# Gate and up products of the inner feed-forward blocks computed with the weights stationary

## The reference, cut to what matters

```
h = rms_norm(x, ffn_norm_w[layer])
gu = h @ w_gate_up[layer]
x = x + (silu(gu[..., :2816]) * gu[..., 2816:]) @ w_down[layer]
```

## Time and profile before

| | |
|---|---|
| three runs | 1253.15, 1253.07, 1252.16 us; median 1253.07 |
| the profiled execution's own time | 1253.0 us |
| its span, first to last instruction | 1251.8 us |
| matmuls on TensorE | 7066, busy 1243.3 us (99%) |
| VectorE, ScalarE, GpSimd | busy 65%, 55%, 11% |
| mean granted TensorE clock | 0.999 of full speed |

### The profile page before, as it was taken

One profiled execution on the slowest core, in us unless ns is written; L12 is line 12 of the kernel. 1 busy time (PEld: TensorE's weight loads), 2 busy tenths in 40 slices (PEclk: granted clock), 3 DMA queues, 4 the chain that ended last, 5 costly groups with the idle time before them and its releaser, 6 DMA issues.

```text
span 1251.8 us, 17456 instructions
## 1 busy us (share of the span) xinstructions
PE 1243.3 (99%) x7066; PEld 1032.8 (83%) x7066; DVE 814.0 (65%) x1114; ACT 691.2 (55%) x1046; POOL 140.8 (11%) x119
## 2 busy tenths in 40 slices
PE   9999999999999999999999999999999999999997
PEld 8888888888888888888888887888888888888886
DVE  5657755566788556655567888846875765755654
ACT  6665644443778645444447755546855363645543
POOL 1130000000221200000000322000320000211112
PEclk9999999999999999999999999999999999999999
DMA  8755466865454648555545534333456544565652
GB/s 296 229 158 185 147 223 202 267 187 164 152 164 157 216 155 253 190 181 178 181 148 188 184 121 150 119 103 102 135 202 235 173 147 133 170 214 171 204 169 85
DMA packets 127697, 220.18 MB, mean 176 GB/s; under 512 B 8336, under 2 KB 71184, under 8 KB 127616
## 3 DMA queue, kind: packets, MB, share of 16 engines
q1 hardware_dynamic: 123360, 205.95, 51.2%
q0 software_dynamic: 2672, 10.20, 2.4%
q10 hardware_dynamic: 1584, 2.92, 0.6%
HBM read 215.88 MB, written 3.15 MB: 175 GB/s over the span
## 4 chain that ended last, share of the span: by engine, by line
PE 96%; issue 1%; DMA 1%; ACT 1%; DVE 0%; POOL 0%; ACTq 0%; SPq 0%; POOLq 0%
PE ps L403 25%; PE ps L405 25%; PE ps L404 25%; PE ps L503 5%; PE ps L504 2%; PE ps L820 1%; PE ps L420 1%; PE ps L677 1%; PE ps L808 1%; PE ps L1058 1%; PE ps L1073 1%; DMA ar<-in_mem 0%; PE ps L779 0%; DMA raw<-in_w_gate_up 0%; PE ps L607 0%
## 5 line engine op out<-in xcount | busy, mean ns | idle before, releaser
L1615 DVE TENSOR_TENSOR spl<-raw,spl 128x1024 fp32r<-128x1024 f32 x387 | 477.4, 1258 | 102.8 <-ACT spl L1106 101.2
L1106 ACT CAST spl<-raw 128x1024 fp32r<-128x1024 f32 x387 | 400.1, 1050 | 181.7 <-PE ps L405 88.1
L403 PE MATMUL ps<-spl,xs 128*128 128x512 f32 x928 | 371.3, 400 | 0.0
L405 PE MATMUL ps<-spl,xs 128*128 128x512 f32 x928 | 362.2, 390 | 0.0
L404 PE MATMUL ps<-spl,xs 128*128 128x512 f32 x928 | 361.4, 389 | 0.0
L405 PEld LDWEIGHTS ps<-spl,xs 128*128 128x128 f32 x928 | 174.1, 188 | 37.4
L403 PEld LDWEIGHTS ps<-spl,xs 128*128 128x128 f32 x928 | 174.4, 188 | 35.8 <-issue 1.5
L404 PEld LDWEIGHTS ps<-spl,xs 128*128 128x128 f32 x928 | 174.5, 188 | 34.1 <-issue 0.5
L403 PE MATMUL ps<-spl,ys 128*128 128x512 f32 x496 | 198.5, 400 | 0.1
L405 PE MATMUL ps<-spl,ys 128*128 128x512 f32 x496 | 193.7, 391 | 0.0
L404 PE MATMUL ps<-spl,ys 128*128 128x512 f32 x496 | 193.2, 390 | 0.0
(11 more groups left out here) (329 smaller groups left out, 1146.5 us busy)
## 6 DMA issues: line engine op xcount, KB each, us to landing
raw<-in_w_in SPq DMA_DIRECT2D x112, 512.0 KB, 3.7
raw<-in_w_gate_up SPq DMA_DIRECT2D x176, 256.0 KB, 4.1
raw<-in_mlp_w SPq DMA_DIRECT2D x64, 512.0 KB, 4.4
raw<-in_w_down SPq DMA_DIRECT2D x44, 512.0 KB, 4.5
raw<-in_w_out SPq DMA_DIRECT2D x24, 512.0 KB, 4.1
raw<-in_xattn_wk SPq DMA_DIRECT2D x8, 512.0 KB, 4.0
raw<-in_xattn_wv SPq DMA_DIRECT2D x8, 512.0 KB, 4.4
raw<-in_w_branch_gdn SPq DMA_DIRECT2D x8, 512.0 KB, 3.2
```

The source lines that it names most:

```text
L403: self.do.matmul(bank, xh, hi, start=start, stop=False)
L405: m = self.do.matmul(bank, xl, hi, start=False, stop=stop)
L1106: self.do.copy(self.k.spl[:, u % NH, 0, :], self.k.raw[:, u % NR, :]).then_inc(*self.up("hi", (u,)))
L1615: self.do.tensor_tensor(lo, self.k.raw[:, u % NR, :], hi.bitcast(F32), ALU.subtract).then_inc(*self.up("lo", (u,)))
```

## The change

In blocks 1 to 9 of both layers (the second to the tenth of 11) the gate and up product is made by `cols_gated`: a unit's 128x128 weight blocks are stationary, four to a channel block (two of gate, two of up). Each high block meets both input parts in one matmul of 2 x 256 columns, then each low block the high input in one of 256. A block now holds four PSUM banks. `gate_sums` copies and adds the halves; the norm factor, now along the free axis, is multiplied in by GpSimd from a row tile `rr` ahead of the tanh; `gate_act` finishes the activation with GpSimd's second multiplication; `gate_split` writes `ys`. The transposes of these blocks are gone. `gate_row` makes `rr` once in a layer: VectorE spreads r / 2 over 128 columns, TensorE transposes that twice, ScalarE copies it out. `hs` moves out of `gated` into the addition of the finished down product to x (`norm_prep`), in all blocks. Blocks 0 and 10 keep the form of before.

```diff
+    def cols_gated(self, blk, src, k, xin, ready):
+
+        x = self.k.x[xin]
+        if k == 0:
+            self.pair = [self.hold(blk, f) for f in range(4)]
+        u, hi, lo = self.next_unit(src(k))
+        self.wait_ge(*self.at("lo", u))
...
+        for f in range(4):
+            b = self.pair[f].rearrange("p (l n) -> p l n", l=2)
+            for j in range(2):
+                kt = 2 * k + j
+                self.do.matmul(b, hi[:, j, f * P:(f + 1) * P], x[:, :, kt, :], start=(kt == 0), stop=False)
+        for f in range(4):
+            for j in range(2):
+                kt = 2 * k + j
+                m = self.do.matmul(self.pair[f][:, 0:T], lo[:, j, f * P:(f + 1) * P], x[:, 0, kt, :], start=False, stop=(kt == 7))
...
+        if k == 3:
+            for f in range(4):
+                self.let((blk, f), "dm", *blk, f)
+
+    def gate_row(self, l):
+        v = self.s2(f"rr{l}")[:, 0, 256:512]
+        b = self.hold("rr", l)
+        for t in range(2):
+            self.wait_ge(*self.at("dm", "rr", l, t))
+            m = self.do.transpose(b[:, t * P:(t + 1) * P], v[:, t * P:(t + 1) * P], self.ident())
+        m.then_inc(*self.up("mx", ("rr", l)))
+        self.let(("rr", l), "am", "rr", l)
...
+    def gate_row(self, l):
+        self.wait_ge(*self.at("mx", "rr", l))
+        self.do.copy(self.s(f"rr{l}")[:, 0:T], self.ps("rr", l)[:, 0:T]).then_inc(*self.up("am", ("rr", l)))
+
+    def gate_sums(self, l, b):
+        for f in range(4):
+            self.wait_ge(*self.at("mm", "gu", l, b, f))
+            self.fresh(f"ac{b}")
+            self.do.copy(self.s(f"ac{b}")[:, f * T:(f + 1) * T],
+                         self.ps(("gu", l, b), f)[:, T:2 * T]).then_inc(*self.up("am", ("guc", l, b, f)))
+
+    def gate_act(self, l, b):
+        v = self.s2(f"act{b}")[:, 0, :]
+        self.wait_ge(*self.at("pm", "gz", l, b))
+        self.do.activation(v, v, ACT.Tanh).then_inc(*self.up("am", ("gt", l, b)))
...
-            self.do.tensor_tensor(v, self.ps(acc, t, j), v, ALU.add).then_inc(*self.up("rx", ("x", n, t, j)))
+            if acc[0] == "fd":
+                self.wait_ge(*self.at("dm", "hs", acc[1], t))
+                a = self.do.scalar_tensor_tensor(v, self.ps(acc, t, j), self.small(f"hs{acc[1]}{t}", 1), v, ALU.mult, ALU.add)
...
+    def gate_row(self, l):
+        v = self.s2(f"rr{l}")[:, 0, 256:512]
+        self.fresh(f"rr{l}")
+        for t in range(2):
+            self.wait_ge(*self.at("dm", "hr", l, t))
+            self.do.tensor_scalar(v[:, t * P:(t + 1) * P], self.ident(), 0.0, self.small(f"hr{l}{t}", 1), ALU.mult,
+                                  ALU.add).then_inc(*self.up("dm", ("rr", l, t)))
+
+    def gate_sums(self, l, b):
+        for f in range(4):
+            c = self.s(f"ac{b}")[:, f * T:(f + 1) * T]
+            self.wait_ge(*self.at("am", "guc", l, b, f))
+            self.do.tensor_tensor(c, self.ps(("gu", l, b), f)[:, 0:T], c, ALU.add).then_inc(*self.up("dm", ("gu", l, b, f)))
+
+    def gate_act(self, l, b):
+        v = self.s2(f"act{b}")[:, 0, :]
+        self.wait_ge(*self.at("am", "gt", l, b))
+        self.do.scalar_tensor_tensor(v, v, 1.0, self.s2(f"ac{b}")[:, 0, :], ALU.add, ALU.mult).then_inc(*self.up("dm", ("gv", l, b)))
...
+    def gate_sums(self, l, b):
+        v, g = (self.s2(f"{n}{b}")[:, 0, :].rearrange("p (f n) -> p f n", f=2) for n in ("act", "ac"))
+        self.wait_ge(*self.at("am", "rr", l))
+        self.fresh(f"act{b}")
+        self.wait_ge(*self.at("dm", "gu", l, b, 1))
+        self.do.tensor_tensor(v, g, bm(self.s(f"rr{l}")[:, 0:T], 2), ALU.mult).then_inc(*self.up("pm", ("gz", l, b)))
+
+    def gate_act(self, l, b):
+        self.wait_ge(*self.at("dm", "gv", l, b))
+        self.wait_ge(*self.at("dm", "gu", l, b, 3))
+        v = self.s2(f"act{b}")
+        self.do.tensor_tensor(v[:, 1, :], v[:, 0, :], self.s2(f"ac{b}")[:, 1, :], ALU.mult).then_inc(*self.up("pm", ("go", l, b)))
...
+        if turned_block(b):
+            E.take(f"ac{b}")
+            for k in range(4):
+                E.cols_gated(("gu", l, b), lambda k: wg[:, 2 * k:2 * k + 2, :, b * 256:(b + 1) * 256], k, "xs", turned(n))
+                if k == 3:
+                    E.gate_sums(l, b)
+                E.ahead()
...
+                if b == 1 and k == 1:
+                    E.ffn_turn(l, 0)
+                    E.give("act0", ("mx", "ft", l, 0))
+                    E.gate_row(l)
+            ffn_down(E, l, b - 1, wd)
+            continue
...
+        if turned_block(b + 1):
+            if n0 == 0:
+                E.gate_act(l, b + 1)
+            else:
+                E.gate_split(l, b + 1)
```

More of the change, by code:

```diff
@@ L512, in cols_joined, with cols_gated @@
                 self.let((blk, f), "dm", *blk, f)
+    def cols_gated(self, blk, src, k, xin, ready):
+        x = self.k.x[xin]
[5 more added lines that the diff above has]
+            for t in range(2):
+                self.wait_ge(*self.at(*ready(t, 2 * k + j)))
+        for f in range(4):
[4 more added lines that the diff above has]
+        for f in range(4):
+            for j in range(2):
+                kt = 2 * k + j
+                m = self.do.matmul(self.pair[f][:, 0:T], lo[:, j, f * P:(f + 1) * P], x[:, 0, kt, :], start=False, stop=(kt == 7))
+            keys = [("w", u)] if f == 3 else []
+            if k == 3:
+                keys.append((*blk, f))
+            if keys:
+                m.then_inc(*self.up("mm", *keys))
+        if k == 3:
[9 more added lines that the diff above has]
+        self.let(("rr", l), "am", "rr", l)
     def rows_open(self, w, kts):
@@ L1787, in factors, with gate_split @@
             self.do.tensor_tensor(b, a, r, ALU.mult).then_inc(*self.up("dm", ("hs", l, t)))
+    def gate_row(self, l):
+        v = self.s2(f"rr{l}")[:, 0, 256:512]
+        self.fresh(f"rr{l}")
+        for t in range(2):
+            self.wait_ge(*self.at("dm", "hr", l, t))
[10 more added lines that the diff above has]
+        self.do.scalar_tensor_tensor(v, v, 1.0, self.s2(f"ac{b}")[:, 0, :], ALU.add, ALU.mult).then_inc(*self.up("dm", ("gv", l, b)))
+    def gate_split(self, l, b):
+        x = self.k.x["ys"][:, :, 2 * (b % 4):2 * (b % 4) + 2, :]
+        self.wait_ge(*self.at("xh", "ft", l, b))
+        self.do.tensor_tensor(x[:, 1], self.s2(f"act{b}")[:, 1, :].rearrange("p (f n) -> p f n", f=2), x[:, 0].bitcast(F32),
+                              ALU.subtract).then_inc(*self.up("xl", ("ft", l, b)))
     def gated(self, l, b):
@@ L1796, in gated @@
             self.wait_ge(*self.at("dm", "g0", l, b, t))
-            self.wait_ge(*self.at("dm", "hs", l, t))
-            self.do.scalar_tensor_tensor(o, v, self.small(f"hs{l}{t}", 1), w[:, 256:512], ALU.mult,
-                                         ALU.mult).then_inc(*self.up("dm", (blk, t)))
+            self.do.tensor_tensor(o, v, w[:, 256:512], ALU.mult).then_inc(*self.up("dm", (blk, t)))
     def ffn_turn(self, l, b):
@@ L2349 @@
 ahead turn turn_in squares_in norm_prep norm_scale rows_half acc_done evac gated gate_evac relu squares sums power factors merge let_merged
-up_sum up_relu warm load_first first_half load_ident load_rows load_tables load_second load_con load_gain load_slot load_kept load_narrow load_gate half weights keep
+up_sum up_relu gate_row gate_sums gate_act gate_split warm load_first first_half load_ident load_rows load_tables load_second load_con load_gain load_slot load_kept load_narrow load_gate half weights keep
 mem_keys mem_keys_turn ma_norm ma_turn ma_scores softmax ma_sums eight ma_eight ma_out out_norm
@@ L2605, in ffn @@
         E.take(f"act{b}")
+        if turned_block(b):
+            E.take(f"ac{b}")
+            for k in range(4):
+                E.cols_gated(("gu", l, b), lambda k: wg[:, 2 * k:2 * k + 2, :, b * 256:(b + 1) * 256], k, "xs", turned(n))
+                if k == 3:
+                    E.gate_sums(l, b)
+                E.ahead()
+                if l == 0 and k == 3 and b == 2:
+                    E.take("mem2a", "mem2b")
+                    E.load_second()
+                if l == 0 and k == 3 and b == 5:
+                    E.load_con()
+                if b == 1 and k == 0:
+                    E.take(f"rr{l}")
+                if b == 1 and k == 1:
[4 more added lines that the diff above has]
+            continue
         k0 = 0
@@ L2615, in ffn @@
             E.ahead()
[L2616 to L2624, removed]
         if b:
             ffn_down(E, l, b - 1, wd)
+    E.give(f"rr{l}", ("pm", "gz", l, NB - 2))
     E.take("g_" + after)
```

20 lines of the change are left out of this document (17 added, 3 removed).

## The result

| | before | changed |
|---|---|---|
| median of the runs | 1252.76 us (1252.16 to 1253.15, 6 runs) | 1258.38 us (1255.86 to 1260.62, 6 runs) |
| ratio | 1 | 1.0044, 95% interval 1.0034 to 1.0054 |
| the profiled execution's own time, span | 1253.0, 1251.8 | 1260.62, 1259.3 |
| mean granted clock | 0.999 | 0.996 |

The change makes the kernel slower by 0.44%, or 5.6 us between the medians. Its runs lie up to 4.8 us apart, those of before 1.0.

The account below looks back on a forecast made before the run. TensorE was taken to bound the kernel. The terms -8.1 (transposes) + 2.7 (matmul shape) + 8.7 (row of norm factors) + 0.3 (multiply-add) = +3.6 us on 1253.0 gave 1256.6 us, range 1252.0 to 1262.0.

Parts of the forecast that it names:

- What bounds the kernel: Whole kernel: TensorE, busy 99% of the span; other engines' work counts only when TensorE has to wait for it.
- Transposes, -8.1 us: Nine blocks in each of two layers: removing four transposes and the slower start behind them saves 0.45 us a block.
- Shape, +2.7 us: Gate and up products: 8 x 512 plus 8 x 256 columns a unit cost 0.037 us more than 12 x 512.
- The upper end of 6.9: Gate and up products: at the MLP's 512-and-256 pair price throughout, 2.82 us a unit, 6.9 us more.
- The formula weighed against it: TensorE matmul price of columns / 2.4 + 2.5 ns, giving 0.6 us extra for the new shape in place of 2.7.
- Waits, +4.4 and +4.3 us: Block 1, layers 0 and 1: TensorE's two row transposes wait for VectorE's source; together 8.7 us more.
- Factor on the sum, +0.3: Finished down product: addition to x becomes a multiply-add, 751 ns in place of 684; 0.3 us more.
- Costed at nothing: Blocks' results and banks come in time; VectorE gets some 2.5 us more per 16.8, from 59% busy to about 74%.
- The sign named for late results: Starts of successive down products: 16.5 us apart where 16.79 stood; above that, results or banks come late.
- Rival 1, the clock falls,: New stalls in both layers: TensorE's clock falls, some 2.5 us lost each; 1259.1 with one, 1261.6 with two; chance 0.22.
- Rival 2, a short stall: Block 1, ScalarE's queue: chain only 2.0 us a layer; 1251.9 us, or 1249.2 with free 256s; chance 0.15.
- Rival 3, late results: Each block: a down product or bank waits on VectorE or ScalarE; one microsecond a block gives 1274.6; chance 0.08.

Follow-up runs that it names:

- early source's kernel: Changed kernel with VectorE making the norm row's source a block earlier, within block 0; 1250.39 us, ratio to before 0.9981.
- paired order: Changed kernel with the norm row's source made within block 0 and each 512-column gated matmul followed by its 256; 1252.85 us, ratio 1.0000.

## Why the prediction was right, step by step

- **What bounds the kernel.** Right. In every version TensorE was busy for 99% of the span, and the versions differ by TensorE's work, its waits and its clock alone.
- **Transposes, -8.1 us.** Not tested by themselves, but the blocks' distance fits: 16.61 where -0.45 and the measured shape give 16.59. In the early source's kernel, where no wait is left, -3.1 for the blocks, 0.3 for the factor on the sum and 0.4 for the row (0.2 in each layer) make -2.4, measured -2.3.
- **Shape, +2.7 us.** Undersized: 4.5 within the products, and 5.0 by the blocks' distance if the transposes are worth their 8.1. The trace gives 0.119 for a 256 in a row, where I took 0.117, and eight 512s behind a 256 lose 0.03 us, where I had 0.009 for the first of them alone. The upper end of 6.9, the pair's price, is what the paired order costs (2.82 a unit). The formula weighed against it, by the Trainium skill, TensorE: Matmul & The Clock Gate, section Back-to-back issue gap, was further off. The estimate worked out from it is 0.7 us (four more matmuls in a unit at 2.5 ns each, 72 units); the 0.6 of the prediction comes from the rounded 216 and 109.
- **Waits, +4.4 and +4.3 us.** Mechanism and place as predicted, VectorE's L1862 named as the releaser. 4.8 in layer 0, 0.1 of it by the clock that fell while the last transpose ran; 2.6 in layer 1, because TensorE reached that place later in relation to VectorE and ScalarE than the sum, which took VectorE's time from before unshifted, allowed: 4.3 + 3.6 - 5.3 = 2.6. With the wait alone in the kernel before they are 4.2 and 3.7.
- **Factor on the sum, +0.3.** Open between 0 and 0.3.
- **Costed at nothing.** Right: no bank and no down product waited. The sign named for late results, more than 16.5 us between down products, did appear (16.61), but by the shape and with no idle time: the results of block 1 are complete at 166.6 (L1879) and due at 174.63. VectorE's busy share went to 106.7 / 173.5 = 62%, where I had allowed 74%. Of GpSimd's two multiplications in a block only the first slows a split of VectorE. The second slows none and is itself longer:

```profile
158.83 1.29 POOL L2317 TENSOR_TENSOR ar<-ar 128x512 f32<-128x512 f32 x1 [23.17 <-ACT ar L1309]
159.24 1.96 DVE L1678 TENSOR_TENSOR spl<-raw,spl 128x1024 fp32r<-128x1024 f32 x1
...
162.86 1.22 DVE L1678 TENSOR_TENSOR spl<-raw,spl 128x1024 fp32r<-128x1024 f32 x1
163.02 2.21 POOL L2323 TENSOR_TENSOR ar<-ar 128x512 f32<-128x512 f32 x1 [2.90 <-DVE ar L1874]
```

  That is 0.7 us a block for VectorE in place of the 1.7 of the prediction. (Its 3.5 for three undisturbed splits holds, 3.49 at 166.52, but not as three times 1.22, which is 3.7.)
- **Rival 1, the clock falls,** was given 0.22 and taken as an alternative to the forecast; it happened in both layers of the profiled execution, at 1.7 us each where I had priced 2.5. The mean clocks of the six runs, 0.996 to 0.998 against 0.999 in the profile of before, suggest falls in most of them. It stands beside the forecast terms: without it the profiled execution would have taken 1257.2, which is what both kernels with work inside the wait came to, 1257.2 after the overlong work is taken off and 1257.6. How much of the median is the clock stays open. Against those two kernels it is about 1 us. But two more of the six runs have the mean clock of the profiled execution, 0.996, and are 1.3 and 1.8 us faster than it, and the fastest, 1255.86, lies below 1257.2. So the waits too differ from run to run, and the share may be nearer 3.
- **Rival 2, a short stall,** was half right in layer 1, for another reason than the one given. **Rival 3, late results,** didn't occur.

The forecast of 1256.6 was 1.8 us below the median and 4.0 below the profiled execution. For the latter the parts are +3.4 for the clock, +2.3 for the blocks (shape), -1.3 for the waits (0.4 more in layer 0, 1.7 less in layer 1) and -0.3 for the factor on the sum, which the account doesn't need, together 4.1. That the forecast came as near as it did is in part luck: shape and waits erred in opposite directions, by 2.3 and 1.3, and the clock's falls, left out of the forecast, weighed less in the median than in the profiled execution or were made up for by shorter waits. Right without luck are the path, TensorE, the place of the waits and their releaser, and the sign.

## What to carry to other kernels

When the bounding engine gets a small job whose input another engine makes, look at what stands ahead of that input in the other engine's own order: two operations of 0.28 us cost 2.6 to 4.8 us a layer here, since they stood behind a chain that the bounding engine itself had just begun, and making them some lines earlier turned 0.44% slower into 0.2% faster. Matmuls of half the columns are not half the price: before trading transposes for them, price the change of length and the run of short ones separately, and group equal lengths.

## What the runs showed of the hardware

- A fall of the clock can come after the idle stretch is over. TensorE began again at 150.53 and the half clock set in at 150.70; in layer 1 it began at 487.18, was at full clock at first and at half from 488.62. The busy matmuls that followed ran at 1.2 GHz for 3.4 us each time. With the wait alone in the kernel before, the fall of layer 1 came within the wait, at 488.13. With TensorE's work inside the waits, which left 1.3 us idle or none, the clock held. The Trainium skill, TensorE: Matmul & The Clock Gate, section HAM oscillation, warns of idle gaps within kernels; these traces agree, with falls behind or within idle stretches of 4.2, 3.7, 3.5 and 2.5 us.
- Idle time isn't needed: 3.6 us of smaller matmuls without a gap were followed by a fall in one execution of a kernel (855.2 us), which cost 1.6 us. The other four executions of the same program have mean clocks of 0.999 and 1.0, which speak against such a fall in them.
- A 512 in fp32r costs 0.227 us in a run of its kind. Eight of them behind 256s cost 0.03 more in all, a single one between two 256s 0.01, and a 256 0.119 in a run and 0.117 in a pair. Why, these runs don't tell; a version with fewer weight columns wasn't tried.
